# Rotary attention queries and keys kept channel-major, with partners swapped by DMA, in a fused hybrid layer

## What is computed

```python
def rope(x, pos):
    ang = pos[:, None] * inv_freq[None, :]
    x1, x2 = x[..., :half], x[..., half:]          # half = 32 channels
    return jnp.concatenate([x1 * cos - x2 * sin, x2 * cos + x1 * sin], axis=-1)
...
qh = rope(qb.reshape(bsz, s, 8, 64), pos)
kh = rope(kb.reshape(bsz, s, 2, 64), pos)
scores = jnp.einsum('bnqhgd,bnkhd->bnhgqk', qc, kw) * (64 ** -0.5)
p = jax.nn.softmax(jnp.concatenate([scores, sink], axis=-1), axis=-1)[..., :-1]
```

## Time and profile before

| | before |
|---|---|
| median of 3 runs | 2073.44 us (2072.71 to 2074.47) |
| the profiled execution | 2070.44 us |
| its span on the core | 2068.6 us |
| granted TensorE clock, mean | 0.983 of full speed |
| TensorE matmul busy | 1995.7 us (96%) |
| VectorE busy | 1605.7 us (78%) |
| ScalarE busy | 996.8 us (48%) |
| GpSimd busy | 565.5 us (27%) |

### The profile page before, as it was taken

The page is one execution under the profiler, slowest core; times in us unless marked ns, Lnnn a source line. Parts: engine busy times, 40 slices in busy tenths (PEclk is TensorE's granted clock), DMA queues, the critical chain, the costliest instruction groups (busy, mean ns, idle before and its releaser), DMA issues.

```text
span 2068.6 us, 56649 instructions
## 1 busy us (share of the span) xinstructions
PE 1995.7 (96%) x22633; PEld 1565.0 (76%) x22633; DVE 1605.7 (78%) x5423; ACT 996.8 (48%) x3144; POOL 565.5 (27%) x841
## 2 busy tenths in 40 slices
PE   7589999999999999999999999999999999999995
PEld 6367777788778788778778877778877878877773
DVE  6898777788777778777778777777877777877773
ACT  6655444545454545444444545454544454444432
POOL 0222223232323233223223222323222323322221
PEclk9799999999999999999999999999999999999997
DMA  9001100111110111110011111011111011111001
GB/s 358 29 24 54 45 26 21 43 45 44 44 34 22 34 44 44 44 44 20 27 44 44 44 44 34 16 40 44 44 44 34 23 34 45 44 44 44 24 13 41
DMA packets 35513, 92.74 MB, mean 45 GB/s; under 512 B 9209, under 2 KB 13618, under 8 KB 35250
## 3 DMA queue, kind: packets, MB, share of 16 engines
q1 hardware_dynamic: 34818, 89.11, 13.3%
q10 hardware_dynamic: 432, 0.01, 0.0%
HBM read 71.28 MB, written 17.83 MB: 43 GB/s over the span
## 4 chain that ended last, share of the span: by engine, by line
PE 91%; DVE 4%; ACT 2%; issue 1%; DMA 1%; SPq 0%; POOL 0%; POOLq 0%; ACTq 0%; DVEq 0%
PE bank L502 32%; PE bank L509 19%; PE bank L694 16%; PE bank L517 10%; PE bank L662 2%; PE bank L638 1%; PE bank L651 1%; PE bank L437 1%; DVE w_raw L1434 1%; PE bank L557 1%; PE bank L534 1%; PE bank L539 1%; ACT w_raw L980 1%; PE bank L590 1%; DVE qkv L1054 1%
## 5 line engine op out<-in xcount | busy, mean ns | idle before, releaser
L502 PE MATMUL bank<-xt_half,w_raw 128*128 128x128 f16 x11904 | 731.3, 219 | 0.0
L502 PEld LDWEIGHTS bank<-xt_half,w_raw 128*128 128x128 f16 x11904 | 692.3, 98 | 28.2 <-issue 5.1
L509 PE MATMUL bank<-w_raw,xt_half 128*128 128x512 f16 (+1 forms) x2232 | 434.6, 347 | 11.6 <-ACT xt_half L754 9.6
L1054 DVE SCALAR_TENSOR_TENSOR qkv<-conv_in,cols,qkv 128x128 f32<-128x128 f32 x1152 | 391.5, 383 | 3.5
L509 PEld LDWEIGHTS bank<-w_raw,xt_half 128*128 128x128 f16 x2232 | 218.5, 99 | 173.0 <-issue 13.7
L694 PE MATMUL bank<-w_o,inv_t 128*128 128x512 f16 x768 | 171.0, 379 | 2.0 <-DVE inv_t L1386 2.0
L694 PE MATMUL bank<-w_o,out_b_half 128*128 128x512 f16 x762 | 169.7, 379 | 0.0
L1052 DVE TENSOR_SCALAR qkv<-conv_in,cols 128x128 f32<-128x128 f32 x384 | 90.9, 282 | 86.3 <-ACT halo L788 85.0
L694 PEld LDWEIGHTS bank<-w_o,inv_t 128*128 128x128 f16 x768 | 73.7, 98 | 85.5 <-DVE inv_t L1386 2.4
L694 PEld LDWEIGHTS bank<-w_o,out_b_half 128*128 128x128 f16 x762 | 73.3, 98 | 82.6
L754 ACT ACTIVATE xt_half<-bank,small 128x128 f16<-128x128 f16 x496 | 131.2, 415 | 3.8 <-DVE small L1478 3.6
(11 more groups left out here) (257 smaller groups left out, 3549.7 us busy)
## 6 DMA issues: line engine op xcount, KB each, us to landing
x_in<-in_x_dram SPq DMA_DIRECT2D x32, 512.0 KB, 3.5
x_in<-near_scratch SPq DMA_DIRECT2D x32, 512.0 KB
y_out<-in_x_dram SPq DMA_DIRECT2D x32, 512.0 KB, 3.5
out_dram<-y_out SPq DMA_DIRECT2D x32, 512.0 KB, 2.8
w_raw<-in_w_in_dram SPq DMA_DIRECT2D x8, 768.0 KB, 10.5
w_raw<-in_w_in_dram SPq DMA_DIRECT2D x16, 256.0 KB, 10.5
w_o<-in_w_out_dram SPq DMA_DIRECT2D x8, 512.0 KB, 12.3
w_raw<-in_w_in_dram SPq DMA_DIRECT2D x8, 384.0 KB, 10.6
```

The costliest lines, as they stand in the source:

```text
L502: last = mm(dst[:, 128 * b:128 * b + 128], w_half[:, c, ws, col:col + 128], xt_half[:, xs, c, :], start=(c == 0 and ws + xs == 0), stop=(c ...
L509: last = mm(dst[:, 0:n_col], xt_half[:, xs, c, :], w_half[:, c, ws, col:col + n_col], start=(c == 0 and ws + xs == 0), stop=(c == NC - 1 a ...
L1054: last = v.scalar_tensor_tensor(dst, conv_in[:, b, i:i + TOK], tap, dst, ALU.mult, ALU.add)
```

## The change

Four things change.

1. QB and the keys of KVB are projected channel-major. QB becomes four pieces of 24 matmuls of 128 columns; KVB becomes 24 of 128 columns (keys) and 24 of 136 (values, a, b). The partner of a channel then lies in another partition, 32 away. SyncE fetches the partners with four DMAs from SBUF to SBUF (`swap_halves`) for the keys and four for the queries. The transposes and ScalarE's copies are gone. The cosines and sines are tables of 192 relative positions, loaded and transposed once at the start; the keys of the last chunk are rotated a second time for their place in the next window (`k_prev`).
2. VectorE does V's tap 1 and the row sums before the block inversion, where it did tap 1 behind it and the row sums among its operations.
3. `near_scratch` holds each block twice, so that each copy is read by 8 partitions.
4. For this, w_in's QB columns are loaded in another order, in two DMAs for each 128 rows (seven loads where there were five), and the heads' order in the softmax is changed.

```diff
             def step(t, p, mix, proj, prep):     # SyncE
-                    sp.dma_start(near_dram, m_near.rearrange("p h n -> p (h n)")).then_inc(near_stored, 16)
...
+                    for s in range(NEAR_COPIES):
+                        sp.dma_start(copies[s], m_near.rearrange("p h n -> p (h n)")).then_inc(near_stored, 16)
...
-                if proj:
-                    done(sp, q_rot_ready, m)
-                    sp.dma_start(rot_tab[:, :], rotary[bass.ds(t * TOK, TOK), :]).then_inc(rot_loaded, 16)
...
+                if proj:
+                    done(sp, kv_raw_ready, t)
+                    swap_halves(k_sw, k_raw, k_swapped)
...
                 if prep and mix:
                     done(sp, to_ready, m)
                     sp.dma_start(x_in[:, :], x[0, bass.ds((t + 1) * TOK, TOK), :]).then_inc(x_loaded, 16)
+                    done(sp, q_raw_ready, t)
+                    swap_halves(rot_sw, rot_in, q_swapped)
```

```diff
+            def swap_halves(dst, src, event):
+                for s in range(4):
+                    sp.dma_start(dst[32 * s:32 * s + 32], src[32 * (s ^ 1):32 * (s ^ 1) + 32]).then_inc(event, 16)
```

```diff
                 if proj:                         # VectorE
                     convolve(t, FILL_V, [0], v_turned if mix else None, m)
-                if mix:
-                    inversion = invert_base(m)
-                    for _ in range(8):
-                        next(inversion)
+                    convolve(t, FILL_V, [1])
+                if mix:
                     done(dve, exp_ready, m)
                     v.tensor_tensor(row_sum, row_sum, sink_arg, ALU.add).then_inc(soft_link, 1)
-                    next(inversion)
...
-                    for _ in inversion:
+                    for _ in invert_base(m):
                         pass
                 if proj:
-                    convolve(t, FILL_V, [1])
                     next(gate_steps)
```

```diff
+            def rotate_queries(t):               # GpSimd
+                done(pool, q_raw_ready, t)
+                done(pool, scores_ready, t - 1)
+                g.tensor_tensor(q_t[:, :, :], rot_in, over_heads(cos_t[:, 64:192], 4), ALU.mult)
+                pool.wait_ge(q_swapped, (t + 1) * 64)
+                g.tensor_tensor(rot_sw, rot_sw, over_heads(sin_t[:, 64:192], 4), ALU.mult).then_inc(rot_link, 1)
+                pool.wait_ge(rot_link, ROT_LINKS * t + 4)
+                g.tensor_tensor(q_t[:, :, :], q_t[:, :, :], rot_sw, ALU.add).then_inc(q_t_ready, 1)
```

More of the change, by code:

```diff
@@ L425, in _ @@
             last.then_inc(setup_turned, 1)
+            pe.wait_ge(rot_loaded, 4 * 16)
+            for n in range(4):
+                last = nc.tensor.transpose(heads(5)[:, n, :], rhs[:, n, :], ident)
+            last.then_inc(tables_turned, 1)
             def turn_x(n):
@@ L504, in fill @@
                                               stop=(c == NC - 1 and ws == 1))
-                        else:
-                            (col, n_col), per = FILL_ROWS[f], NC // (2 if f == FILL_KVB else 4)
-                            for c in range(per * b, per * b + per):
+                        elif f == FILL_ZA:
+                            for c in (2 * b, 2 * b + 1):
+                                for xs, ws in ((0, 0), (0, 1), (1, 0)):
+                                    last = mm(dst[:, :], xt_half[:, xs, c, :], w_half[:, c, ws, COL_ZA:COL_ZA + 512],
+                                              start=(c == 0 and ws + xs == 0), stop=(c == NC - 1 and xs == 1))
+                        else:
+                            for c in range(NC):
                                 for xs, ws in ((0, 0), (0, 1), (1, 0)):
-                                    last = mm(dst[:, 0:n_col], xt_half[:, xs, c, :],
-                                              w_half[:, c, ws, col:col + n_col], start=(c == 0 and ws + xs == 0),
-                                              stop=(c == NC - 1 and xs == 1))
+                                    last = mm(dst[:, 128:KV], xt_half[:, xs, c, :],
+                                              w_half[:, c, ws, COL_KVB + 128:COL_KVB + KV],
+                                              start=(c == 0 and ws + xs == 0), stop=(c == NC - 1 and xs == 1))
                         if (f, b + 1) not in PIECES:
@@ L612, in step @@
                 last.then_inc(q_turned, 1)
-                fill(2)
-                done(pe, q_rot_ready, m)
-                done(pe, decay_arg_ready, m)
-                for c in range(4):
-                    last = nc.tensor.transpose(heads(2)[:, c, :], q_rot[:, 128 * c:128 * c + 128], ident)
-                last.then_inc(qr_turned, 1)
-                done(pe, k_rot_ready, m)
-                done(pe, sq_ready, m)
-                for kv in range(2):
-                    last = nc.tensor.transpose(heads(3)[:, kv, :], k_rot[:, kv, :, :].rearrange("p d n -> p (d n)"), ident)
-                last.then_inc(kr_turned, 1)
-                fill(2)
+                fill(4)
                 done(pe, q_t_ready, m)
@@ L735, in _ @@
             act.dma_start(sinks_raw, sw_sinks.broadcast_to([128, SW_HEADS])).then_inc(heads_loaded, 16)
+            for n in range(4):
+                at, col = CHUNK * (n % 2), 64 * (n // 2)
+                act.dma_start(rot_rows[:, n, :, :], rotary[at:at + TOK, col:col + 64].unsqueeze(1).broadcast_to(
+                    [TOK, 2, 64])).then_inc(rot_loaded, 16)
             def normalise(n):
@@ L808, in small_fill @@
                 done(act, fill_ready[FILL_KVB], t)
[L809 removed]
+                done(act, k_win_ready, t - 1)
                 done(act, g_ready, t - 1)
@@ L939, in step @@
                 if prep:
-                    done(act, q_rot_ready, t)
+                    done(act, q_t_ready, t)
                     normalise(t + 1)
@@ L1417, in _ @@
             link(v.tensor_single_scalar(norm_abs.bitcast(I32), cols[:, 48:56].bitcast(I32), 0x7FFFFFFF, ALU.bitwise_and))
+            dve.wait_ge(tables_turned, 1)
+            for i, table in enumerate((cos_t, sin_t)):
+                v.tensor_copy(table[:, 0:128], heads(5)[:, 2 * i, :])
+                last = v.tensor_copy(table[:, 128:192], heads(5)[:, 2 * i + 1, 64:128])
+            last.then_inc(tables_ready, 1)
             done(dve, x_turned, 0)
```

142 lines of the change are left out of this document (72 added, 70 removed).

## The result

The changed kernel takes 2105.55 us (median of 4 runs, 2105.27 to 2105.67), the kernel before in the same session 2073.95 (2072.71 to 2074.86). The ratio is 1.0149, 95% interval 1.0136 to 1.0161: slower by 31.6 us. The profiled execution of the change took 2105.67 us with a span of 2103.9, 35.3 us more than the span before, at the same granted clock (0.983).

What follows compares the result with a forecast made beforehand. TensorE was taken as the bound, never standing still in a steady step, with VectorE close behind. From the profiled 2070.4 us, plus 46 for 30 steps at 1.55 each, minus 1 for the rest: 2115 us, range 2052 to 2148.

Steps and rivals of the forecast that it cites:

- TensorE's own work: TensorE, each steady step: transposes removed, narrower QB and KVB matmuls added; 0.42 us less per step, 13 us in 31 steps.
- The wait for the exponentials: VectorE after V's tap 1, ahead of the row sums: about 1.3 us idle until ScalarE's exponentials end.
- The inversion: VectorE's block inversion, now started after the row sums: 7.9 us long, with bounds 7.0 and 8.2.
- The cosine product on tap 2: GpSimd's cosine product of the queries falls on V's tap 2 on VectorE, ahead of update(4), and holds it 1.1 us.
- The swap: Queries' swap: four issues at 0.33 us and a landing of about 1.8; GpSimd's sine product about 3.1 us after the copy.
- the sines come late: Sign that the forecast is wrong: GpSimd's sine products come late, TensorE stays the only bound and 13 us are gained.
- couple(5) late: VectorE, held on tap 3 and gate operations: couple(5) ends at 1059.6, wanted by TensorE at 1058.02; 1.55 us per step.
- The rest: Outside the steady steps: last step 2.3 us less, start 1.3 us more, entered as -1 us.
- Last step: TensorE's 9.4 us wait for the softmax shrinks by 1.9 to 2.7 us, taken as 2.3.
- Start: Four table transposes and four copies ahead of the first tile: 0 to 2 us more, taken as 1.3.
- Faster, 2056: Rival, chance 0.28: GpSimd's operations miss the taps and the inversion takes 7.0 us; TensorE's 13 us are gained, 2056 us.
- Weight loads: Rival, chance 0.01: 96 more narrow TensorE matmuls each pay a 98 ns weight load, 9 us per step, 2360 us.

Runs made afterwards that it cites:

- e11: e1 with K's tap 0 moved behind the two scalings of the inverse on VectorE: 2061.0 us, ratio 0.9945 to the kernel before.
- e3: The changed kernel with GpSimd's three long operations on the queries cut from 512 columns to 4, queries not rotated: 2064.1 us, ratio 0.9953.
- e1: The changed kernel with VectorE's old order (inversion at once, row sums among its operations, V's tap 1 behind it): 2067.2 us, ratio 0.9970.
- e2: The kernel before with only VectorE's new order (V's tap 1 and row sums ahead of the inversion): 2175.4 us, ratio 1.0491.
- e10: The changed kernel with two of the four DMAs that swap the queries issued by ScalarE instead of SyncE: 2106.3 us, ratio 1.0158.
- e5: The changed kernel with GpSimd's cosine product of the queries put behind the wait for their swap: 2103.6 us, ratio 1.0143.
- e7: e1 with GpSimd's sine product and add of the queries each split into two halves of 256 columns: 2071.0 us, ratio 0.9981.

## Why the prediction was right

It said 2115 us, slower; 2105.6 was measured. The mechanism is the one forecast, with the following steps.

*TensorE's own work.* -0.42 us per step forecast, -0.36 measured (61.32 to 60.96, e11). QB's matmuls take 56 ns (72 in 4.02 us) and the 136-column ones 59 (24 in 1.42), as forecast:

```profile
1037.99 0.95 PE bank L550 x8
1038.94 1.42 PE bank L542 x24
```

*The wait for the exponentials* was put at 1.3 us of idle time and is 0.84 in a steady step. *The inversion* was put at 7.9 us and takes 7.54. Both were somewhat too large. Together they make TensorE late by 0.23 us per step (e3 against e11).

*The cosine product on tap 2.* Forecast 1.1 us, measured 2.15 - 1.13 = 1.02 (the earlier trace rows and the row above). update(4) starts 2.93 us after couple(4) (1070.45 to 1073.38); it was 1.91. Right, and this is the largest piece: TensorE's wait of 1.0 us in 32 tiles. That GpSimd does it is shown by e3, and that the order brought it there by e1 and e2. The Trainium skill (SBUF — State Buffer, "SBUF: two separate sides") says that VectorE and GpSimd share one port pair, that whoever starts first keeps it for the whole instruction, and that this touches VectorE's operations with two SBUF inputs or in a two-port mode. The traces agree with the holding: a 128x4 operation takes up to 1.25 us, until the very end of GpSimd's, the one-input L1068 takes 1.24, and L1187 and L1194, which read PSUM, never take over 0.23 us in any of the 13 kernels. GpSimd is held in turn: in e1 the add takes 1.60 us where it begins while VectorE's L1079, with two inputs from SBUF, is in work, and 1.27 beside the copy L1184, which reads PSUM. Which mode an operation ran in, no trace here shows.

*The swap.* The step that was sized wrongly was "four issues at 0.33 us [...] and a landing of about 1.8 us [...] some 3.1 us after the copy". Four issues take 2.41 us, 0.6 each, and the landing is 2.3 us in the median; the sine began 3.85 to 3.92 us after the cosine in 17 of 31 steps and 4.1 to 5.15 in the others. The 0.33 came from the earlier trace rows, a single load of x from DRAM. That "the sines come late" was one of the prediction's own signs of being wrong, with the 13 us gained after all. They did come late, by some 0.8 us and more, and nothing was gained, because they held VectorE ahead of update(5) in place of couple(5).

*couple(5) late.* This consequence fell. Counted from the step's first 18 matmuls and put in the old step's times (16.98 us less), update(4) starts at 1056.40, where 1057.1 was forecast, and couple(5) ends at 1057.72, where 1059.6 was forecast: ahead of the 1058.02 at which the old step wanted it. The products came behind couple(5) and held L1118 and L1121, so that it was update(5) that was late, by 0.45 us in 18 steps. e10 shows that this difference of place was worth nothing. My term of 1.55 us per step rests on the late couple(5); measured are 1.16, and they are made otherwise. Against e11, whose TensorE does the same work without a wait, the changed kernel's step is 1.52 us longer: 1.10 before the matmul that needs update(4), 0.29 before the one that needs update(5), 0.13 before the inversion's first. Take off the 0.36 saved and the 1.16 are there. So the largest piece was forecast as it is, and that the total came out near is in part luck: a delay at couple(5) that didn't come stood in for two smaller ones elsewhere. From update(4) to update(5) TensorE has 3.6 us of its own work (the two e11 rows below), VectorE takes 4.1 with its two holdings (1073.71 to 1077.83, ends of the two L1194), and the 0.5 between them is the wait.

```profile
1052.56 0.28 PE bank L567 x8
...
1056.15 0.38 PE bank L576 x8
```

*The rest.* Last step: the wait for the softmax is 5.9 us in place of 9.4, 3.5 less where 2.3 were forecast, but the stretch from the last L537 group to the end came out even. In it the granted clock was at 0.50 for 41.5 us, in the kernel before for 36.0; how much of the 3.5 us that took back, no run singles out. Start: 1.6 for 1.3. The forecast's terms are 46 for the steps and -1 for the rest, the measured ones 33.6 and 1.6: 12 us too much in the steps, 2.6 too little in the rest, 10 in all.

*The rivals.* "Faster, 2056" described e11 rather well: 2061, with the same TensorE bound. Its condition (update(4) done in time) is met with the old order, which the change doesn't have. Weight loads cost nothing, as the 56 ns show.

## What to carry to other kernels

When an engine's order is changed, list not just who waits for whom but which operations will run at the same time as GpSimd's long ones. In these traces an SBUF-only operation on VectorE is as long as what is left of GpSimd's current one, however small it is, so such a moment belongs where a PSUM read, an idle wait or an operation that nobody is waiting for stands (e11), and never ahead of a result that the bounding engine wants. A change that removes work from the bounding engine and reorders another should be measured in its two halves: here one gained 0.3% (0.55% once a tap was moved) and the other, put on top, lost 1.9%, and the loss hid the gain. The halves don't add up, though: the order alone, on the kernel before, lost 4.9% (e2), as it met another rotation and the lower clock. And a moved operation has to be followed to the next result that is queued behind its new place (e5).

## What was not expected of the hardware

- A swap by four DMAs from SBUF to SBUF lands at different delays in steps of the same code: the sine begins 3.9 us after the cosine in 13 steps of e1 and 4.0 to 5.2 in 18. The late ones are those in whose first 3 us a 16 KB packet of the queue q8, "instruction", begins. That it is the cause is likely and not tested.
- Issuing such a DMA takes SyncE 0.6 us, against 0.33 us for a 512 KB load of x; ScalarE needs 1.42 us for two.
- A wait of TensorE can cost more than itself: in e2, with 1.96 us of wait at update(4), the granted clock fell to half for 3.4 us in 18 steps, 1.5 us each. In e5, with waits of up to 2.0 us at L1348, it fell once. With the 1.0 us of the changed kernel it stayed at 1.00 in all of its steady steps.
- Splitting a GpSimd operation of 512 columns into two of 256 costs at least 0.14 us and didn't shorten the time that VectorE was held (e7).
